# Column-wise norm with lent weight buffers, the residual moved to the eleventh pair of experts, and a later scatter, in a decoder layer with 32 experts

## What is computed

```python
x2 = layer_norm(DEEPNORM_ALPHA * x1 + h, ln2_g, ln2_b)   # (x - mu) * rsqrt(var + eps) * g + b
logits = x2 @ w_router + b_router                        # top 4 of 32, softmax over them: gates
h = x2[rows of the expert] @ w_gate_up[e] + b_gate_up[e] # 1024 -> 2048
y = ((clip(u) + 1) * glu(g)) @ w_down[e] + b_down[e]     # 1024 -> 1024
out = layer_norm(DEEPNORM_ALPHA * x2 + sum of gates * y, ln3_g, ln3_b)
```

## Time and profile before

| what | value |
|---|---|
| median of 3 runs | 1204.78 us |
| span of the profiled execution, first to last instruction | 1202.1 us |
| median less span (work around the span) | 2.7 us |
| PE busy | 1146.8 us (95%) |
| DVE / ACT / POOL busy | 219.4 / 133.3 / 49.7 us |
| DMA moved | 446.63 MB, mean 372 GB/s |

### The profile page before, as it was taken

How to read it: one execution, slowest core, us unless ns; L and a number is a source line. 1 busy time by engine, 2 the same in 40 slices (tenths; PEclk the granted TensorE clock), 3 DMA queues, 4 the chain that set the end, 5 groups by cost and what they waited for, 6 DMA issues and landing times.

```text
span 1202.1 us, 12962 instructions
## 1 busy us (share of the span) xinstructions
PE 1146.8 (95%) x5354; PEld 522.3 (43%) x5354; DVE 219.4 (18%) x559; ACT 133.3 (11%) x281; POOL 49.7 (4%) x56
## 2 busy tenths in 40 slices
PE   9999999999999999999999999898989899999986
PEld 7686747754434343433434343333333333333322
DVE  1232122224211111121111111111111111111113
ACT  2133111222100000010000000000000000000001
POOL 0232002010000000000000000000000000000001
PEclk9999999999999999999999999999999999999998
DMA  9953334398999999999999999999999999999995
GB/s 350 323 204 141 133 112 157 122 373 326 429 429 427 427 414 429 428 429 430 427 429 427 427 428 429 429 430 427 428 428 430 429 429 427 429 430 429 427 429 215
DMA packets 55698, 446.63 MB, mean 372 GB/s; under 512 B 10304, under 2 KB 11472, under 8 KB 30192
## 3 DMA queue, kind: packets, MB, share of 16 engines
q1 hardware_dynamic: 53200, 440.49, 88.3%
q10 hardware_dynamic: 2464, 5.66, 1.3%
HBM read 445.06 MB, written 1.07 MB: 371 GB/s over the span
## 4 chain that ended last, share of the span: by engine, by line
PE 62%; DMA 35%; DVE 2%; issue 1%; SPq 0%; ACT 0%
DMA ring<-in_w_gate_up 32%; PE bank L1693 21%; PE bank L1333 9%; PE bank L1742 9%; PE bank L1320 8%; DMA ring<-in_w_down 3%; PE bank L1577 3%; PE bank L1638 2%; PE bank L1653 1%; PE bank L1367 1%; PE bank L1718 1%; PE bank L1792 1%; PE bank L1731 1%; PE bank L1519 1%; PE bank L1497 1%
## 5 line engine op out<-in xcount | busy, mean ns | idle before, releaser
L1693 PE MATMUL bank<-ring,PT 128*64 128x512 f32 x1792 | 396.5, 594 | 29.9 <-DMA ring<-in_w_gate_up 29.9
L1693 PEld LDWEIGHTS bank<-ring,PT 128*64 128x64 f32 x1792 | 125.9, 137 | 295.3 <-issue 235.4
L1182 DVE TENSOR_SCALAR reg_k<-bank 128x512 f32<-128x512 f32 x32 | 22.1, 691 | 449.9 <-PE bank L1693 444.1
L1320 PE MATMUL bank<-reg_bc,ring 128*128 128x256 f32 x448 | 99.6, 381 | 0.0
L805 ACT ACTIVATE reg_v<-reg_k 128x512 f32<-128x512 f32 x30 | 18.9, 630 | 689.3 <-DVE reg_k L1182 689.3
L1742 PE MATMUL bank<-reg_q,NCt 128*64 128x512 f32 x400 | 92.0, 602 | 0.0
L1320 PEld LDWEIGHTS bank<-reg_bc,ring 128*128 128x128 f32 x448 | 84.4, 190 | 14.1 <-issue 3.2
L1742 PE MATMUL bank<-reg_bc,NCt 128*64 128x512 f32 x400 | 90.1, 592 | 0.0
L1577 PEld LDWEIGHTS bank<-L,reg_a 128*128 128x128 f32 x512 | 62.9, 196 | 24.8 <-issue 23.5
L1577 PE MATMUL bank<-L,reg_a 128*128 128x128 f32 x512 | 69.3, 288 | 1.0 <-DVE L L1096 0.7
L1213 DVE COPY reg_v<-bank 128x512 f32<-128x512 f32 x28 | 19.4, 692 | 269.0 <-PE bank L1742 269.0
(11 more groups left out here) (232 smaller groups left out, 709.0 us busy)
## 6 DMA issues: line engine op xcount, KB each, us to landing
ring<-in_w_gate_up SPq DMA_DIRECT2D x114, 2048.0 KB, 23.3
reg_bc<-in_w_down SPq DMA_DIRECT2D x26, 2048.0 KB, 20.7
reg_q<-in_w_down SPq DMA_DIRECT2D x25, 2048.0 KB, 19.2
ring<-in_w_down SPq DMA_DIRECT2D x8, 2048.0 KB, 18.9
ring<-in_w_in SPq DMA_DIRECT2D x5, 2048.0 KB, 17.1
reg_kv<-in_w_gate_up SPq DMA_DIRECT2D x5, 2048.0 KB, 18.0
ring<-in_w_down SPq DMA_DIRECT2D x9, 1024.0 KB, 7.3
reg_q<-in_w_gate_up SPq DMA_DIRECT2D x4, 2048.0 KB, 14.2
```

Source lines behind the costliest of these rows:

```text
L1182: nc.vector.tensor_scalar(gbuf, banks[0][:, :], LIMIT, None, ALU.min).then_inc(g_ready, 1)
L1320: last = mm(B(name)[:, a * T:(a + 1) * T], w[:, k, c:c + P], src[:, k, :], start=(k == 0), stop=(k == KD - 1))
L1693: last = mm(ps[half * CAP:(half + 1) * CAP, :], xgT[:, k, i * CAP:(i + 1) * CAP], w[:, j, col:col + HALF], start=(opens and k == 0), stop= ...
```

## The change

1. **Norm by columns.** x2hat = (x - mu) * rstd, without g and b, is made by ACT alone for all tokens, in place in `reg_v`. `gather` takes x2hat, and `evac_xgT` applies g and b while it leaves the bank: four ACT operations of 128x128 with a column of g and of b as scale and bias, in place of one copy of 128x512. For pair 0 ACT takes blocks 2, 3, 1, 0 and DVE 4 to 7. POOL's and DVE's gain and bias steps go, and so do the loads of g and b as rows; as columns they are loaded early (`lncol`, group `wo0`). The norm 3 loads move behind the last piece.
2. **Two more lent buffers.** `lent` becomes three buffers of 1 MB: k-block 0 of expert 0 in `reg_a`, block 1 in `reg_k`, block 6 of expert 1 in `x_nat`. Chunk (0,0) leaves the list, the opening has 59 chunks, the first is (1,3), `OPEN` goes from 3 to 5 pairs. The first product takes 2 to 7, 1, 0. `sig`, `ysb`, `repT` move from `reg_v` to `reg_a`; the output tile y3 moves to `reg_v`.
3. **Base in pair 10.** `BASE_PAIR` goes from 6 to 10. x2 isn't there as a tensor, so alpha*x2 is made from x2hat: POOL makes diagonals of alpha*g and alpha*b, PE spreads them over the partitions by products with ones, DVE multiplies, PE adds.
4. **Scatter.** `final_down` for the last expert has nothing in between; then both scatters of tile 0, then both of tile 1.

```diff
-BASE_PAIR = 6
+BASE_PAIR = 10
-OPEN = 2 * NSLOT // CH
-OPENING = ([(i, c) for i in range(2) for c in range(GUC)] + [(i, c) for i in range(2) for c in range(GUC, CH)]
+OPEN = 5
+OPENING = ([(1, 3), (0, 1), (0, 2), (0, 3), (1, 0), (1, 1), (1, 2), (0, 4), (0, 5), (1, 4), (1, 5)]
            + [(e, c) for e in range(2, OPEN * 2) for c in range(CH)])
-RINGED = OPEN * 2 * CH // NSLOT - OPEN * 2
+OPENED = [len(range(n, len(OPENING), NSLOT)) for n in range(NSLOT)]
...
+        lent = {(0, 0): reg_a[:, :], (0, 1): reg_k[:, :], (1, 6): x_nat[:, :, :].rearrange("p a d -> p (a d)")}
...
                     load_half(0, 1, slot_in[0])
-                    load_half(NSLOT, 0, ahead_in)
+                    load_half(NSLOT, 0, ahead_in[0])
+                    wait_evacuated(sp, ("wo1", 1))
+                    load_lent(1, 6)
+                    sp.wait_ge(ln_out, TT)
+                    load_lent(0, 0)
                     continue
                 if n == NSLOT - 1:
-                    sp.dma_start(lent, chunk_source(0, 0)[:, 0:1, :]).then_inc(lent_in, 16)
+                    load_lent(0, 1)
...
+            for n in (1, 2, 3):
+                for j in range(2):
+                    sp.wait_ge(opened, 2 * n - 1 + j)
+                    load_half(NSLOT + n, j, slot_in[n] if j else ahead_in[n])
+            sp.wait_ge(opened, 7)
+            load_half(NSLOT + 4, 0, ahead_in[4])
+            wait_opening(4)
+            load_half(NSLOT + 4, 1, slot_in[4])
+            for n in (5, 6):
+                wait_opening(n)
+                load_chunk(*OPENING[NSLOT + n], NSLOT + n)
+            wait_opening(0)
             load_half(NSLOT, 1, slot_in[0])
...
             for c in range(CH):
-                wait_opening(OPEN * 2 * CH - NSLOT + c)
+                wait_opening((OPENED[c] - 1) * NSLOT + c)
                 load_chunk(OPEN * 2, c, c)
...
             def evac_xgT(half, m):
                 act.wait_ge((xgTa_done, xgTb_done)[half], m)
-                nc.scalar.activation(xgT[:, 4 * half:4 * half + 4, :],
-                                     (xy_ps, tr_ps)[half][:, :].rearrange("p (k c) -> p k c", k=4),
-                                     ACT.Copy).then_inc((xgTa_sb, xgTb_sb)[half], 1)
+                for j in range(4):
+                    k = 4 * half + j
+                    last = nc.scalar.activation(xgT[:, k, :], (xy_ps, tr_ps)[half][:, j * P:(j + 1) * P], ACT.Identity,
+                                                scale=lncol[:, 4, k:k + 1], bias=lncol[:, 5, k:k + 1])
+                last.then_inc((xgTa_sb, xgTb_sb)[half], 1)
...
+            def scaled_residual():
+
+                dve.wait_ge(h_ready, 2 * BASE_PAIR + 1)
+                for half in range(2):
+                    cols = slice(half * HALF, (half + 1) * HALF)
+                    dve.wait_ge(gain_done, half + 1)
+                    if half > 0:
+                        dve.wait_ge(scaled_used, half)
+                    for tt in range(TT):
+                        last = nc.vector.tensor_tensor(scaled_x2[tt], xy_ps[:, :], x2hat[:, tt, cols], ALU.mult)
+                    last.then_inc(scaled_ready, 1)
...
             def base(p):
 
+                pe.wait_ge(diag_ready, 1)
+                pe.wait_ge(y_sb, p * 2)
+                for half in range(2):
+                    rows = slice(4 * half, 4 * half + 4)
+                    if half > 0:
+                        pe.wait_ge(scaled_ready, half)
+                    mm(xy_ps[:, :], one, diag[:, 0, rows, :].rearrange("p k f -> p (k f)"),
+                       start=True, stop=True).then_inc(gain_done, 1)
+                    for tt in range(TT):
+                        mm(acc[tt][half][:, :], one, diag[:, 1, rows, :].rearrange("p k f -> p (k f)"),
+                           start=False, stop=False, skip_group_check=True)
+                    pe.wait_ge(scaled_ready, half + 1)
+                    for tt in range(TT):
+                        last = mm(acc[tt][half][:, :], ident, scaled_x2[tt], start=False, stop=False, skip_group_check=True)
+                    last.then_inc(scaled_used, 1)
...
-                for tt in range(TT):
-                    for half in range(2):
-                        mm(acc[tt][half][:, :], K[:, C_AID:C_AID + P], x2[:, tt, half * HALF:(half + 1) * HALF],
-                           start=False, stop=False, skip_group_check=True)
                 pe.wait_ge(cand_ready, 1)
...
-                final_down(p, 1, tr_ps, hT_last, first_scatter)
-                scattered(0, tiles=(1,))
-                pe.wait_ge(y_sb, p * 2 + 2)
-                for done in scatter(1):
-                    done.then_inc(tile_done, 1)
+                final_down(p, 1, tr_ps, hT_last)
+                pe.wait_ge(y_sb, p * 2 + 1)
+                for tt in range(TT):
+                    scattered(0, tiles=(tt,))
+                    if tt == 0:
+                        pe.wait_ge(y_sb, p * 2 + 2)
+                    for done in scatter(1, tiles=(tt,)):
+                        done.then_inc(tile_done, 1)
```

## The result

The changed kernel took 1207.7, 1209.3 and 1211.6 us beside 1204.5 for the kernel before: ratio 1.0042, 95% interval 1.0028 to 1.0055. A fourth execution in a slow state took 6812.5 us and is compared with nothing; with it the median of the four is 1210.4, without it 1209.3. It is slower by 0.3% to 0.4%; I had said 1206.4, no difference that can be told.

A forecast was written before the change was run, and what follows sets the result against it. The stream of weight loads was taken to set the end. Span 1202.1 - 2.9 + 1.6 + 3.4 - 0.5 = 1203.7, with 2.7 around it 1206.4 us; range 1200.5 to 1209.3.

The forecast's parts named there:

- the sum for the stream: Weight stream up to its last piece: -2.9 at (3,1), +1.6 at (10,3), +3.4 in the base pair.
- three places: Loads (3,1), (10,3) and the one behind chunk 4 in the base pair, each predicted to meet an empty queue.
- Lent buffers: 2 MB more ahead works once; the queue runs dry about 331 us, (3,1) lands at 340.4: -2.9 us including PE's start.
- PE's start: First product at the opening gathers: about 0.5 us earlier, range -0.6 to +0.5.
- Evacuation and the step from nine slots to six: Split evacuation delays down 0.6 us per pair in pairs 1 to 4; (10,3) issued at 550.7, gap +1.6 us.
- Base: Pair 10: PE's work 7.2 us longer, leaving 4.3 us where a load needs 7.7: gap +3.4 us (2.8 to 4.4).
- the row of 11.5 us: Trace row of the kernel before: time to landing of the load behind chunk 4 in its base pair, at 641 us.
- the reserve: A 2 MB load's landing time beyond 7.7 us, from loads queued ahead; 3.8 us in the old base pair.
- Scatter and tail: End of the kernel: last down product without a scatter inside, tile 0 0.7 us earlier; -0.5 us (-0.7 to 0).
- The rule that I set aside: Skill page's fixed DMA cost of about 2.0 us, against 2.8 from the 7.7 row; by the page the estimate is 1204.0.
- The slower rival: ACT's split evacuation stalls down in pairs 1 to 4 by s each; decides from s = 0.8 (1207.2 us); 31%.
- bounds, 1204.0 to 1207.2: Span given for the sum with its bounds, chance 47%.

The follow-up runs named there:

- a1_no_xnat: Changed kernel without the lent buffer x_nat, so 1 MB less is loaded ahead: 1209.3 us, ratio 1.0048 to the kernel before.
- a3_evac_dve: Changed kernel with the four evacuations of gather(0) on DVE instead of ACT in all pairs: 1207.4 us, ratio 1.0026 to the kernel before.
- f2_filler2: Changed kernel with three zero products filling PE's waits for candidates (two) and tables (one) in the base: 1205.9 us, ratio 1.0006 to the kernel before.
- a0_same: Changed kernel unaltered, measured again in a second series: 1207.8 us (1205.8 to 1211.9), ratio 1.0031 to the kernel before.
- f1_filler: Changed kernel with two zero products in PE's wait for the candidates in the base: 1207.4 us, ratio 1.0017 to the kernel before.
- d3_before_open5: Kernel before with OPEN 5 instead of 3 (nine slots used to expert 9), nothing else: 1205.0 us, ratio 1.0003.
- e1_split_evac: Changed kernel with the base's table steps moved to pair 7 and gather(0)'s evacuations on DVE: 1202.8 us, ratio 0.9983 to the kernel before.
- d4_before_scatter: Kernel before with the scatter change alone: 1204.4 us, ratio 0.9997.

## Why the prediction came out wrong

The step that failed is the sum for the stream: +2.1 us predicted, +4.8 measured. It priced three places and put everything else at nothing, while landings that come late beside code loads cost 3.1 us more in after than in before. And it took the base as one fixed gap of 3.4 us, where the gap measured 3.5 in one execution and 8.0 in another, by how long the clock was at half. The first accounts for the profiled execution (1207.7 where 1206.4 was forecast), the second carries others to 1211.6 and 1211.9. The three dry places themselves, and their sizes in after, were right.

- **Lent buffers: right in size, and in reason as far as after shows.** -2.9 predicted, -3.2 measured at (3,1). The chunk ahead of it landed 5.3 us earlier than before (333.0, before 338.4), the DMA engines moved 66 GB/s from 330 to 332 us and nothing in the next, and 2.1 of the 5.3 were lost there. What the sum didn't say is how long the rest lasts. a1_no_xnat is 2.1 us later ahead of expert 10 and equal at the end: there the landing hangs on the issue of (10,3), not on the stream ahead of it, so what is ahead is given back.
- **PE's start: right.** 0.7 us earlier (284.05; before 284.7), predicted 0.5.
- **Evacuation and the step from nine slots to six: right.** 0.60 us per pair, issue at 550.75 for 550.7, gap 1.8 for 1.6. a3_evac_dve takes it away.
- **Base: the count of work right, the clock wrong.** From the base's start to the product on the candidates, PE took 870.60 - 859.45 = 11.2 us where before it took 627.85 - 623.93 = 3.9: +7.2, as predicted, and a full stream would have landed the load 4.3 us after its issue, as predicted (883.25, the landing before it, + 4.89 - 883.88). So the gap of 3.5 for 3.4 is no luck as to the work. As to the clock it is: the row of 11.5 us that I started from holds 3.4 us at half clock, and the profile of after happens to hold as much. One such stretch costs PE 1.7 us. Without any the gap is 3.1 in f2_filler2, of which 1.0 is a late landing, and with three of them in a0_same it is 8.0. My bounds were 2.8 to 4.4. The windows of the base pair in before show it:

```profile
630.00:635.00 5.00, 4.28 (x28) 3.08 (x28) 1.38 (x11) 0.75 (x2) 0.00 (x0) 0.95 1.02 428
635.00:640.00 5.00, 5.00 (x18) 1.34 (x18) 0.00 (x0) 0.36 (x1) 0.00 (x0) 0.70 0.99 423
```

  The clock is at 0.95 and 0.70 behind a wait of 0.72 us there, too, which is (0.05 + 0.30) x 5 x 2 = 3.5 us at half; the reserve hid it. The change took the reserve away and put a longer wait in (the four alpha*x2 products had covered DVE's table steps). From a0_same to f2_filler2 the ratio falls by 0.25%, 3.0 us, and the medians, which are of different series, by 1.9, though f2_filler2 has more to do. a0_same lies 3.4 us above the kernel before where 1.6 were forecast, so this is at least the size of what its median misses.
- **Code loads: a term I didn't have.** In after, a chunk that follows a dry place by some chunks lands late once more, while the DMA engines stay full. Issues and landings in after (view of DMA issues, narrow windows at 342.81, 346.25 and 887.32), the windows at that time, and the queues between 358.5 and 360:

```profile
ring<-in_w_down SPq DMA_DIRECT2D x1, 2048.0 KB, 11.9
...
reg_q<-in_w_down SPq DMA_DIRECT2D x1, 2048.0 KB, 14.8
...
reg_bc<-in_w_down SPq DMA_DIRECT2D x1, 2048.0 KB, 10.4
```

```profile
355.00:360.00 5.00, 5.00 (x28) 1.59 (x24) 0.00 (x0) 0.00 (x0) 0.00 (x0) 1.00 1.00 426
360.00:365.00 5.00, 5.00 (x26) 1.71 (x24) 0.69 (x1) 0.00 (x0) 0.00 (x0) 1.00 1.01 426
```

```profile
q8 instruction: 1, 0.02, 4.6%
```

  The first two land at 354.8 and 361.1: 6.3 apart instead of 4.9. A code load of 16 KB lies there, one packet on one DMA engine for 4.6% of 16 x 1.5 us = 1.1 us. In after such late landings come at 361.1 (+1.4), 579.7 (+1.5) and 897.7 (+1.2), behind the dry places at 340, 559 and 892; the code loads in between cost 0.1 to 0.2. In before the late landings behind 343 come to 1.6 us together (0.1 to 0.8 each), in after to 4.7 without the two dry places. The difference, 3.1, is what the sum lacks: -3.2 + 1.8 + 3.5 + 3.1 = 5.2, measured 4.8 to 4.9. It isn't chance of one profile: the same count gives 3.8 to 4.8 in all nine profiles with the change (in f1_filler and f2_filler2 with the late part of the dry load) and 1.6 to 2.9 in the five without, the 2.9 in d3_before_open5, which has the longer unrolled part and its four code loads more. My reading is that one DMA engine falls behind by the code load, a chunk counts as landed with its slowest engine, and a dry place levels the engines, so that the next code load counts anew. The Trainium skill ("DMA: Bandwidth & Descriptors", section "Why a DMA increments its semaphore by 16 and not by 1") says that the engines finish independently and only the full count means that all has landed, which fits. It is argued from the rows, not shown by an experiment of its own, and the part on dry places fits badly: e1_split_evac has no dry place at expert 10 and 20 us behind that landing still +1.1 at 577.5 (and +1.3 at 902.4), and a1_no_xnat has no late landing at 361 but +1.5 at 524.7, far from any dry place. What makes one code load count and another not stays open.
- **Scatter and tail: right in sign.** -0.5 predicted; d4_before_scatter has -0.3 once the last store is set aside. In after the end is 1.5 nearer to the last piece (13.8, before 15.3). The rest is that store: 2.6 us and not 3.7, in every profile with the change. Nothing in the prediction had it, and why it is shorter isn't shown.
- **The rule that I set aside.** Three dry loads took 7.6 to 7.9 us, as the row of 7.7 said; the two of f1_filler and f2_filler2, beside a code load, took 9.0 and 8.7. The Trainium skill ("DMA: Bandwidth & Descriptors", section "Anatomy of one DMA — SWDGE (gpsimd) path") gives its fixed cost of about 2.0 us for DMAs that GpSimd issues. My prediction set it against loads that SyncE issues and called that a difference between trace and page; it isn't one. An estimate with that figure and 4.9 in the stream would be 6.9. The measurement decides: some 2.8 for a load of 2 MB here.
- **The rivals.** The slower rival put the risk at the evacuation (s over 0.8 us per pair); s was 0.60. It was slower than forecast through the base and the code loads. The sum's error was in the term for the base, mis-sized (3.4 for 3.5 to 8.0), and in a term that was missing. My "bounds, 1204.0 to 1207.2" weren't the bounds of the terms either: with each term at its lower bound the sum is 1204.7, and 1204.0 is the estimate by the page.

## What to carry to other kernels

Where a stream of loads sets the end, an early gain lasts only to the next place where the queue would run dry: list every such place with its reserve before you count the gain, and keep work that stops PE in pieces smaller than the reserve. Ask for the granted clock in the very window of a stage that you price, since a stage with short waits for another engine may run at half clock in some executions, and a reserve hides that until you spend it. When such waits can't be removed, filling them with products that change nothing can be cheaper than leaving them empty, as it was here.

## What the hardware showed that I had not expected

- TensorE's granted clock fell to half behind waits as short as 0.73 us when small products (96x1, 96x16) lay around them; windows of 5 us showed 0.65 to 0.95. The same kernel had it in different lengths from one execution to the next: four products of 96x512 took 3.68 or 7.07 us. With three zero products in the waits it stayed at 1.00 in the one profile, and the spread of 11 executions was 1.7 us. It also fell behind a wait of 2.67 us in pair 9, and in other profiles the same waits brought no fall.
- A landing may be late by 1.2 to 1.5 us while the DMA share is 1.00 and the rate 426 GB/s: landings, not the rate, tell when PE can go on.
- While POOL makes the two diagonals (798.94 to 802.69 us in after), DVE's product of 128x512 takes 2.40 us, in the same pair of before 0.68. PE waits 2.67 us for what follows it, before 0.41. That the two are linked is read from their times alone. The prediction put the diagonals at nothing, which held only because the next load there still took 18.2 us to land. The rows of after:

```profile
800.84 2.40 DVE L1201 TENSOR_TENSOR reg_k<-reg_k,reg_a 128x512 f32<-128x512 f32 x1
...
798.94 3.75 POOL L630 TENSOR_TENSOR x_nat<-K,lncol 128x1024 f32<-128x1024 f32 x2 [520.11 <-PE bank L1715]
```
